# Small constant products at five norms, and the first queries' chunks in other banks and two places earlier

## The reference, cut to what matters

```
def rms_norm(x, gain):
    xf = x.astype(jnp.float32)
    y = xf * lax.rsqrt(jnp.mean(xf * xf, axis=-1, keepdims=True) + NORM_EPS)
    return (y * gain.astype(jnp.float32)).astype(x.dtype)
...
for layer in range(DEPTH):                       # layer 0: HGRN2 mixer, layer 1: chunked attention
    u = modulate(rms_norm(h, norm_mix[layer]), sh1, sc1)
    ...                                          # mixer or attention, added to h
    u = modulate(rms_norm(h, norm_ffn[layer]), sh2, sc2)
    h = h + g2[:, None, :] * swiglu(u, ffn_w_in[layer], ffn_w_out[layer])
    if layer == N_A_LAYERS - 1:                  # after layer 0: keys and values of layer 1
        k_pad, v_pad = shared_kv(h, c_act, kv_norm, kv_mod_w, kv_mod_b, kv_w)
return rms_norm(h, final_norm)
...
# second block: two gated mixers (mLSTM and long convolutions), then
x = x + rms_norm_2(mix, norm_mix_post)
hm = rms_norm_2(x, norm_mlp_pre)
ff = jnp.square(jax.nn.relu(hm @ w_mlp_in)) @ w_mlp_out
x = x + rms_norm_2(ff, norm_mlp_post)
```

## Time and profile before

| what | value |
|---|---|
| runs (us) | 7352.82, 2252.87, 2250.42; median 2252.87 |
| profiled execution (us) | 2250.53 |
| its span (us) | 2248.4 |
| mean granted TensorE clock, as a share of full speed | 0.981 |
| TensorE matmul busy | 2148.9 us, 96% of the span |
| DVE, ACT, POOL busy | 58%, 40%, 12% |
| chain of waits that ended last | TensorE 85%, DVE 7%, issue 3%, ACT 2%, POOL 1% |

### The profile page before, as it was taken

How to read it: one execution, slowest core, us unless ns; L and a number is a source line. 1 busy time by engine, 2 the same in 40 slices (tenths; PEclk the granted TensorE clock), 3 DMA queues, 4 the chain that set the end, 5 groups by cost and what they waited for, 6 DMA issues and landing times.

```text
span 2248.4 us, 25866 instructions
## 1 busy us (share of the span) xinstructions
PE 2148.9 (96%) x10024; PEld 1720.5 (77%) x10024; DVE 1305.3 (58%) x1938; ACT 893.8 (40%) x1259; POOL 261.4 (12%) x280
## 2 busy tenths in 40 slices
PE   7999999899999989999799999998999998999997
PEld 3887887688888868666688888876578876888885
DVE  7866765543443462485534444487566757555556
ACT  5423243375555545465322222255134333322222
POOL 3000000054444413000000000001410000000000
PEclk9999999899999989999999999999999998999998
DMA  6632321355555523320132223222022222222221
GB/s 225 230 131 94 113 94 57 131 187 188 187 187 187 187 94 114 111 84 29 57 113 94 94 94 104 97 83 75 19 75 103 88 91 75 94 94 94 98 89 38
DMA packets 39484, 247.48 MB, mean 110 GB/s; under 512 B 4927, under 2 KB 5183, under 8 KB 11588
## 3 DMA queue, kind: packets, MB, share of 16 engines
q1 hardware_dynamic: 27940, 191.75, 24.6%
q0 software_dynamic: 8080, 47.79, 6.0%
q10 hardware_dynamic: 3344, 6.29, 0.7%
HBM read 239.52 MB, written 6.29 MB: 109 GB/s over the span
## 4 chain that ended last, share of the span: by engine, by line
PE 85%; DVE 7%; issue 3%; ACT 2%; POOL 1%; DVEq 0%; ACTq 0%; POOLq 0%
PE bank L731 26%; PE bank L733 25%; PE bank L732 25%; PE bank L997 2%; DVE w_lo L1996 2%; PE bank L1115 1%; PE bank L1125 1%; PE bank L1136 1%; PE bank L765 1%; ACT w_hi L1471 1%; PE bank L881 1%; PE bank L875 1%; DVE scr L2031 0%; POOL pool L687 0%; PE bank L1020 0%
## 5 line engine op out<-in xcount | busy, mean ns | idle before, releaser
L731 PE MATMUL bank<-u_hi,w_hi 128*128 128x512 f32 x1708 | 691.9, 405 | 23.5 <-DVE u_lo L2063 9.0
L733 PE MATMUL bank<-u_hi,w_lo 128*128 128x512 f32 x1708 | 670.0, 392 | 0.0
L732 PE MATMUL bank<-u_lo,w_hi 128*128 128x512 f32 x1708 | 669.9, 392 | 0.0
L1996 DVE TENSOR_TENSOR w_lo<-raw,w_hi 128x2048 fp32r<-128x2048 f32 x160 | 366.8, 2293 | 202.8 <-ACT w_hi L1471 202.7
L1471 ACT ACTIVATE w_hi<-raw 128x2048 fp32r<-128x2048 f32 x160 | 305.3, 1908 | 282.5 <-PE bank L733 269.1
L731 PEld LDWEIGHTS bank<-u_hi,w_hi 128*128 128x128 f32 x1708 | 323.8, 190 | 110.4 <-issue 38.7
L733 PEld LDWEIGHTS bank<-u_hi,w_lo 128*128 128x128 f32 x1708 | 323.1, 189 | 69.0
L732 PEld LDWEIGHTS bank<-u_lo,w_hi 128*128 128x128 f32 x1708 | 323.9, 190 | 66.2 <-issue 4.1
L731 PE MATMUL bank<-g_hi,w_hi 128*128 128x512 f32 x772 | 304.5, 394 | 9.1 <-DVE w_lo L1996 6.4
L733 PE MATMUL bank<-g_hi,w_lo 128*128 128x512 f32 x772 | 300.9, 390 | 0.0
L732 PE MATMUL bank<-g_lo,w_hi 128*128 128x512 f32 x772 | 300.9, 390 | 0.0
(11 more groups left out here) (297 smaller groups left out, 2195.9 us busy)
## 6 DMA issues: line engine op xcount, KB each, us to landing
raw<-in_wts SPq DMA_DIRECT2D x180, 1024.0 KB, 4.8
pool<-in_wts POOLq DMA_DIRECT2D x36, 1024.0 KB, 5.2
spectra<-pool ACTq DMA_DIRECT2D x16, 256.0 KB, 2.1
scr<-in_rel POOLq DMA_DIRECT2D x16, 256.0 KB, 3.0
pool<-spectra POOLq DMA_DIRECT2D x16, 256.0 KB, 3.0
H<-in_x ACTq DMA_DIRECT2D x1, 2048.0 KB, 15.0
out<-H SPq DMA_DIRECT2D x8, 256.0 KB, 2.0
pool<-in_window POOLq DMA_DIRECT2D x1, 1024.0 KB, 8.4
```

What stands on the lines that cost most here:

```text
L731: pe.matmul(out, lh, rh, start=start, stop=False, skip_group_check=True)
L732: pe.matmul(out, lh, rl, start=False, stop=False, skip_group_check=True)
L733: return pe.matmul(out, ll, rh, start=False, stop=stop, skip_group_check=True)
L1996: dve.tensor_tensor(w_lo[RING[w]][:, :], raw[W_STREAM[w] % raw_ring][:, :], w_hi[RING[w]][:, :].bitcast(F32), ALU.subtract).then_inc(lo_do ...
```

## The change

A new helper `busy(b, count)` makes `count` float32 products of 128x128 of two constants, the identity and a matrix of ones, into a bank whose last output has been read and whose next one has not begun. `norm` now takes the first output after the norm as `target`, claims its bank, and makes ten such products before the narrow ones, four between them and the spread, and nine after the spread. This is at `ffn0`, `kv`, `ffn1` and `post2`. At `mlp_post2` only four are made, between the narrow products and the spread.

The two outputs of query slot 0 go to banks 4 and 5 in place of 0 and 1. ACT's `values(3)` stands behind the eighth rounded chunk. The query steps are taken two places earlier: three of them stand at the place (-2, 0), and none at (3, 2) and (3, 3). ACT's reads of the query outputs come two places earlier too.

```diff
+Q_AHEAD = 2
...
-    out("qq", 8, "act", slots=[("qq", i) for i in range(4)], banks=(0, 1))
+    out("qq", 8, "act", slots=[("qq", i) for i in range(4)], banks=(4, 5, 0, 1, 0, 1, 0, 1))
...
-            def norm(name):
+            def busy(b, count):
+
+                for _ in range(count):
+                    pe.matmul(b[:, 0:P], ident[:, :], ones[:, :], start=True, stop=True)
+
+            def norm(name, target):
                 n = NORM[name]
+                b = claim(target)
+                busy(b, 10)
                 pe.wait_ge(sq_add, 8 * (MAIN[name] + 1))
-                if n:
-                    pe.wait_ge(*released(n - 1))
+                pe.wait_ge(*released(n - 1))
                 norm_cols(n, ssum)
+                busy(b, 4)
                 norm_bc(n)
+                busy(b, 9)
...
-            norm("ffn0")
+            norm("ffn0", FIRST["fi0_0"])
...
             for n in range(24):
-                fill[(n // TB - 2, n % TB)] = queries[n // KC]
+                at = max(n - Q_AHEAD, 0)
+                fill.setdefault((at // TB - 2, at % TB), []).append(queries[n // KC])
...
             mm.then_inc(n_col, 1)
+            pe.wait_ge(*free_of(FIRST[f"mout{MLP_G - 1}"]))
+            busy(bank[PLACE[FIRST[f"mout{MLP_G - 1}"]]], 4)
             norm_bc(NORM["mlp_post2"])
...
-            modulated("mix1", U_MIX1, SC1_1, SH1_1, lambda c: used("vv", 2 + c // 4), lambda x: x == 2 and values(3))
+            modulated("mix1", U_MIX1, SC1_1, SH1_1, lambda c: used("vv", 2 + c // 4), lambda x: x == 3 and values(3))
...
-                    if (g, j) in ((-1, 3), (1, 3), (3, 3)):
+                    if (g, j) in ((-1, 1), (1, 1), (3, 1)):
                         queries((g + 3) // 2)
```

More of the change, by code:

```diff
@@ L1066, in ffn @@
                         slot_out(f"fo{layer}", g - 1, FIRST[f"fo{layer}_{g - 1}"], gcount)
-            norm("ffn0")
+            norm("ffn0", FIRST["fi0_0"])
             ffn("0", U_FFN0, G_FFN0)
-            norm("kv")
+            norm("kv", FIRST["kk"])
             for i in range(4):
@@ L1148, in _ @@
             for n in range(24):
-                fill[(n // TB - 2, n % TB)] = queries[n // KC]
+                at = max(n - Q_AHEAD, 0)
+                fill.setdefault((at // TB - 2, at % TB), []).append(queries[n // KC])
             for j in range(TB):
-                fill[(4, j)] = outs[0]
+                fill[(4, j)] = [outs[0]]
             for g in (5, 6, 7):
-                fill[(g, 2)] = outs[0]
+                fill[(g, 2)] = [outs[0]]
             for at in ((6, 0), (6, 1), (6, 3), (7, 0), (7, 1), (7, 3)):
-                fill[at] = outs[1]
+                fill[at] = [outs[1]]
             for g in range(-2, PAIRS):
@@ L1164, in _ @@
                         pe.wait_ge(at_sc, 4 * B_HEADS)
-                    if (g, j) in fill:
-                        next(fill[(g, j)])
-                    if (g, j) in ((-1, 3), (1, 3), (3, 3)):
-                        assert next(fill[(g, j)], None) is None
+                    for step in fill.get((g, j), ()):
+                        next(step)
                     if TB * g + j >= 1:
@@ L1173, in _ @@
                 pass
-            norm("ffn1")
+            norm("ffn1", FIRST["fi1_0"])
             ffn("1", U_FFN1, G_FFN1)
@@ L1417, in _ @@
                 pass
-            norm("post2")
+            norm("post2", FIRST["mi0"])
             lead = mlp_slot(0)
```

## The result

| | before | after |
|---|---|---|
| first comparison, five runs each: median (us) | 2252.87 | 2240.06 |
| its runs | 2250.42 to 2253.89, and 7352.82 | 2233.70, 2236.21, 2240.06, 2240.43, 2242.87 |
| ratio, 95% interval | | 0.9943 [0.9932, 0.9953] |
| profiled execution (us) | 2250.53 | 2233.70 |
| mean granted clock | 0.981 | 0.992 |

So there are two questions: whether the steps were sized rightly, and why one kernel's times lie 9 us apart.

What follows compares the result with a forecast made beforehand. TensorE, busy for 96% of the span, bounds the kernel, so its waits and slow clock count. Norms 10.5 plus queries 6.5 make 17.0 us off the profiled 2250.53, giving 2233.5; range 2227 to 2245.

Steps and rivals of the forecast that it cites:

- the forecast's own 2228 to 2240: Whole kernel: the range given to the case that the sum comes as worked out, with chance 0.62.
- the sum: Whole kernel: norms 10.5 and queries 6.5 together save 17.0 us; places not edited count 0.
- Does the clock stay up?: At the norms: constant products hold the full clock; a single wait of about 2.7 us is near the edge.
- the prediction's own sign: The forecast is wrong if the clock still reads 0.50 through `ffn0`, `kv` and `ffn1`.
- The norms: At `ffn0`, `kv` and `ffn1`: full-speed narrow products, spread and large products save 4.3, 3.2 and 2.8 us.
- `post2`: At this norm the first large product stays put, waiting for DVE's low part; saves 0.2, ends 0 and 0.5.
- The last norm: At `mlp_post2`: four products cost 0.3 or save up to 1.7 us; taken as 0.
- the larger-gain rival: `kv` gains whole and the last norm runs at full speed: 2227 to 2229, chance 0.07.
- The queries: Query part: waits of 2.65 and 2.50 us and the low clock behind slot 0 go; saves 6.5, ends 3.8 and 7.
- That those idle times would be gone: In the attention: DVE's idle times at (3, 2) and behind it, 1.59 to 1.00 us, would be gone.
- the total: Whole kernel: 17.0 us off the profiled 2250.53 gives 2233.5, with nothing added for the median.
- the clock falls at the norms all the same: At the norms: no gain and late products give about 2247, partly held 2237 to 2243; together chance 0.17.

Runs made afterwards that it cites:

- the second trace: The changed kernel run again unedited for a second profile: median 2234.57, ratio 0.9932; profiled execution 2232.75.
- `norms_only`: The changed kernel with the query part undone, only the constant products kept: 2245.91, ratio 0.9975.
- `queries_only`: The changed kernel without the constant products, only the query part kept: 2249.46, ratio 0.9990.
- `one_column`: The changed kernel with its constant products cut to one column and doubled in number: 2284.31, ratio 1.0144.
- `banks_only`: The kernel before plus only banks 4 and 5 and ACT's new order; no steps moved, no constant products: 2251.52, ratio 0.9997.
- `ahead_only`: The kernel before plus only the query steps moved to (-2, 0); banks and ACT's order as before, no constant products: 2252.21, ratio 0.9999.
- `steady`: The changed kernel with more constant products at the norms, the first MLP output, the last norm and four more waits: 2230.85, ratio 0.9899.
- `steady_no_queries`: `steady` with queries, banks and ACT's order as in the kernel before: 2236.69, ratio 0.9940.

## Why the prediction was right, and where it was not

The forecast of 2233.5 is the profiled execution (2233.70) almost exactly, and the median of the first comparison, 2240.06, lies inside 2227 to 2245 but outside the forecast's own 2228 to 2240 by a hair. That the profiled execution agrees to 0.2 us is luck. Against the sum, the queries, `post2`, the last norm and the mLSTM part gave 3.8 us more than forecast, and two places that the sum left out took 3.6; that execution was also the shortest of its five.

- **Does the clock stay up?** Right in effect, not in full: it fell at `ffn0` and `kv` for 3.4 us, late enough for the nine products to hide most of it. By the prediction's own sign, a clock of 0.50 in those stretches, this part was missed. The argument behind it, that a wait of about 2.7 us is near the edge, did not hold up: the clock held over 3.16 us at `post2`, 2.92 near 1068 (both in the changed kernel) and 2.65 before query slot 0 (`norms_only`), and fell at waits of 2.50 (`norms_only`), 2.33 (`queries_only`, near 1479) and 2.13 (the changed kernel, at 1883). `one_column` shows that it is the wide products that keep it up.
- **The norms**: 3.8, 3.4 and 2.7 against 4.3, 3.2 and 2.8.
- **`post2`**: mis-sized, 1.1 against 0.2. "The first large product stays where it is" was wrong. DVE's low part waits for ACT's rounding, and ACT rounds only behind the root, which the narrow products release. DVE after, for the second of the earlier trace rows:

```profile
1851.78 2.29 DVE L2006 TENSOR_TENSOR w_lo<-raw,w_hi 128x2048 fp32r<-128x2048 f32 x1 [0.89 <-ACT w_hi L1481]
```

  It starts 3.18 us behind the narrow products' start (1848.60) and before 3.84, so the cover itself moved up by 0.66; the 0.5 for the clock makes up the rest. And the clock held over the 3.16 us of nothing, where I took it to fall.
- **The last norm**: 1.7 against 0; it was the larger-gain rival's half that came. It held over the same 1.39 us idle in which it had fallen before.
- **The queries**: 7.4 against 6.5. I had cut for DVE's idle times; TensorE waited for nothing of note there. That those idle times would be gone was too much, as DVE's rows for the earlier trace rows show:

```profile
1014.80 0.76 DVE L2338 SCALAR_TENSOR_TENSOR pool<-bank,scr 128x256 f32<-128x256 f32 x2 [0.59 <-PE bank L1124]
...
1018.40 1.02 DVE L2338 SCALAR_TENSOR_TENSOR pool<-bank,scr 128x384 f32<-128x384 f32 x2 [1.01 <-PE bank L1124]
```

- **The step that failed** is the total: "one of the three runs, 2250.42, is as short as the profiled one, so I add nothing for the median", with the last sentence that clock drops elsewhere "come and go ... with no part in this". They have a part. The sum was taken against a trace in which the clock had held at three uncovered waits (2.92, 2.35 and 2.13 us) and at the start, and in the changed kernel's trace it fell at two of these places: +2.1 (1.6 of it by the low stretch near 53) and +1.5, where the sum has 0. I had the first wait's row and priced it at nothing. The median then lies 6.4 above the profiled execution, where before's is 2.3 above. `queries_only`, `banks_only` and `ahead_only` show it for half of the change, `steady` and `steady_no_queries` from the other side.
- **The rival "the clock falls at the norms all the same"** did not come: groups of ten, four and nine held it or let it down for 3.4 us. The swing that the Trainium skill (TensorE: Matmul & The Clock Gate, A second HAM failure mode: psum-queue depth-cycling) describes for short idles between groups did not show at `ffn1` and `post2`, which read 1.00. One fall and rise each at `ffn0` and `kv`, behind idle times of 0.58 and 0.29 and of 1.33 and 0.29 us, may be of that kind; the second trace has it at `kv` only.
- **Places left with transposes and scores** kept the clock. The changed kernel through (3, 1), (3, 2) and (3, 3), with no large product in about the last 6 us:

```profile
1000.00:1010.00 10.00, 10.00 (x81) 6.28 (x79) 7.50 (x23) 7.43 (x23) 0.29 (x2) 1.00 0.19 77
```

  No trace here has a low stretch between 950 and 1060 us, with (3, 2) and (3, 3) cut to small products in the changed ones. The rule of the Trainium skill (TensorE: Matmul & The Clock Gate, Part 4: PE-mode transpose) that transposes do not count as busy did not show at these places, where scores stand between them.

What stays open: at which waits the runs near 2241 have their added low clock, since no profile fell on one; and why a wait of a given length holds the clock in one kernel or execution and drops it in another. That only the shift in time decides at a later wait is not tested.

## What to carry to other kernels

Where TensorE waits for 1.3 to 3 us at full speed, put in products that fill the wait, wide ones, and fewer than fit; count at half speed too, since they are late if the clock falls first. Treat all marginal waits of the kernel together: what was gained at one was in part lost at others, and only with six more places filled did the median pass what the sum had promised. Price a saving against more than one trace, and give the marginal waits that happened to hold a price of their own. Where no trace falls on a long run, compare the mean granted clock of the runs.

## What the runs showed that I had not expected

- One column costs TensorE as much as 128 in float32 (0.26 us for one narrow product, 0.24 for a wide one).
- One-column products do not keep the clock, however busy TensorE is: 23.8 us at 0.50 with 23.80 busy, and +1.4% in the time for 192 such products.
- The loss from a marginal wait is 1.3 to 1.6 us for a low stretch of 3.4 us, and about 3.7 for one of 10.2 near 1540: between 1489 and 1562 `steady` gained 3.9 on before and the changed kernel 0.2.
- Two gains of 4.3 and 3.2 us, each plain in its own trace, gave medians 0.6 below and 0.1 above before, and 0.9990 together.
